# First layer's input projection from its second block on as three products of split operands, with both parts of the first norm counted together

## The reference, cut to what matters

```python
def rmsnorm(x, g, eps=NORM_EPS):
    xf = x.astype(jnp.float32)
    y = xf * lax.rsqrt(jnp.mean(xf * xf, axis=-1, keepdims=True) + eps)
    return (y * g).astype(x.dtype)

def even_mixer(hn, p, ctx, layer_idx):
    ...
    proj = hn @ p['w_in']                       # 1024 x (1536 + 352)
    qa, ka, va, q_down, ckv, kpe = jnp.split(
        proj, [HA * 2 * DA, 2 * HA * 2 * DA, A_COLS, A_COLS + Q_LORA, A_COLS + Q_LORA + KV_LORA], axis=-1)
    ...
    qb = heads(rmsnorm(q_down, p['q_norm']) @ p['w_uq'], HB)
    ckv = rmsnorm(ckv, p['kv_norm'])
    ...

def trunk_layer(h, cond, p, mixer, ctx):
    sh1, sc1, g1, sh2, sc2, g2 = jnp.split(jax.nn.silu(cond) @ p['ada_w'] + p['ada_b'], 6, axis=-1)
    hn = rmsnorm(h, p['norm1']) * (1.0 + sc1) + sh1
    m, ctx_out = mixer(hn, p['mix'], ctx)
    ...
```

## Time and profile before

| | |
|---|---|
| Time before, median of 3 runs | 2240.46 us (2232.99 to 2259.75) |
| Profiled execution, its own time | 2247.07 us |
| Its span in the trace | 2245.3 us |
| PE busy | 2114.6 us, 94% of the span |
| DVE busy | 1097.4 us, 49% |
| ACT busy | 659.0 us, 29% |
| DMA queue of weight loads, share of 16 engines | 20.6% |

### The profile page before, as it was taken

The page is one execution under the profiler, slowest core; times in us unless marked ns, Lnnn a source line. Parts: engine busy times, 40 slices in busy tenths (PEclk is TensorE's granted clock), DMA queues, the critical chain, the costliest instruction groups (busy, mean ns, idle before and its releaser), DMA issues.

```text
span 2245.3 us, 41199 instructions
## 1 busy us (share of the span) xinstructions
PE 2114.6 (94%) x18328; PEld 1776.9 (79%) x18328; DVE 1097.4 (49%) x2006; ACT 659.0 (29%) x1192; POOL 152.2 (7%) x145
## 2 busy tenths in 40 slices
PE   6998999999999999999998879999969999999998
PEld 3544444559999999999996468888945999999998
DVE  3004644426555554244544746777742655555423
ACT  2001433314333333132334423233111333333311
POOL 2000000000000000000002712222000000000000
PEclk8998999999999999999998869999979999999999
DMA  9021643712222211232120000000021222222222
GB/s 325 26 75 57 216 151 113 262 38 76 76 76 76 76 52 53 78 94 76 57 66 7 20 2 3 3 4 3 4 80 38 75 71 74 76 73 59 54 78 73
DMA packets 141505, 163.72 MB, mean 73 GB/s; under 512 B 2368, under 2 KB 106864, under 8 KB 141328
## 3 DMA queue, kind: packets, MB, share of 16 engines
q1 hardware_dynamic: 137872, 148.81, 20.6%
q0 software_dynamic: 3456, 12.28, 1.6%
HBM read 157.32 MB, written 3.75 MB: 72 GB/s over the span
## 4 chain that ended last, share of the span: by engine, by line
PE 87%; DVE 8%; DMA 2%; ACT 1%; issue 1%; POOL 0%; ACTq 0%; SPq 0%; DVEq 0%; POOLq 0%
PE ps L218 82%; DMA ring<-in_ada_w 1%; PE ps L1619 1%; PE ps L1034 1%; DVE work L2160 1%; DMA ring<-in_ffn_up 1%; PE ps L314 1%; DVE work L463 1%; DVE x_lo_r L469 0%; DVE work L2205 0%; PE ps L329 0%; PE ps L1937 0%; PE ps L1919 0%; PE ps L427 0%; DVE work L2196 0%
## 5 line engine op out<-in xcount | busy, mean ns | idle before, releaser
L218 PE MATMUL ps<-x_hi_r,w_lo 128*128 128x320 f32 (+2 forms) x2112 | 497.2, 311 | 4.5 <-ACTq L202 3.5
L218 PE MATMUL ps<-work 64*64 64x64 f32 (+6 forms) x4942 | 388.0, 272 | 31.0 <-ACT work L2080 9.1
L218 PE MATMUL ps<-x_lo_r,w_hi 128*128 128x320 f32 (+2 forms) x1664 | 394.1, 311 | 8.2 <-DVE g_lo L737 8.2
L218 PE MATMUL ps<-x_hi_r,w_hi 128*128 128x320 f32 (+2 forms) x1664 | 393.5, 310 | 0.7 <-issue 0.7
L218 PEld LDWEIGHTS ps<-work 64*64 64x64 f32 (+4 forms) x4942 | 249.4, 150 | 158.7 <-issue 101.0
L218 PEld LDWEIGHTS ps<-x_hi_r,w_lo 128*128 128x128 f32 x2112 | 357.4, 188 | 6.4 <-ACTq L202 3.7
L218 PEld LDWEIGHTS ps<-x_lo_r,w_hi 128*128 128x128 f32 x1664 | 283.2, 189 | 8.8 <-DVE g_lo L737 8.8
L218 PEld LDWEIGHTS ps<-x_hi_r,w_hi 128*128 128x128 f32 x1664 | 281.7, 188 | 1.2 <-issue 1.1
L568 DVE SCALAR_TENSOR_TENSOR work<-ps,par,work 128x511 f32<-128x511 f32 (+1 forms) x188 | 103.4, 550 | 272.3 <-ACT work L702 264.6
L615 DVE TENSOR_TENSOR w_lo<-ring,w_hi 128x1024 fp32r<-128x1024 f32 (+1 forms) x152 | 158.4, 1078 | 98.5 <-ACT w_hi L604 98.5
L702 ACT ACTIVATE work<-ps,par 128x640 f32<-128x640 f32 x88 | 77.8, 884 | 400.8 <-PE ps L218 400.8
(11 more groups left out here) (332 smaller groups left out, 2355.0 us busy)
## 6 DMA issues: line engine op xcount, KB each, us to landing
ring<-in_ada_w SPq DMA_DIRECT2D x24, 2048.0 KB, 8.1
ring<-in_ffn_up SPq DMA_DIRECT2D x44, 1024.0 KB, 7.2
ring<-in_ffn_down SPq DMA_DIRECT2D x16, 1408.0 KB, 7.0
ring<-in_l_w_in SPq DMA_DIRECT2D x11, 1024.0 KB, 5.2
ring<-in_l_w_out SPq DMA_DIRECT2D x4, 2048.0 KB, 9.1
ring<-in_l_w_in SPq DMA_DIRECT2D x3, 2048.0 KB, 7.9
h<-in_xT POOLq DMA_DIRECT2D x1, 2560.0 KB, 14.8
out_yT<-work POOLq DMA_DIRECT2D x2, 768.0 KB, 4.2
```

The source lines that it names most:

```text
L218: return pe.matmul(out, lhsT, rhs, start=first, stop=last)
```

## The change

Block 0 stays as it is. Blocks 1, 2 and 3 are made of three fp32r products each. For that, ACT copies the eight tiles of `hn` to `x_hi` right behind the norm, and DVE, once block 0 is done, subtracts to `x_lo` in place over `hn`; each of the three weight blocks is rounded by ACT in four pieces (`m0_w_hi`) and subtracted by DVE in four (`m0_w_lo`), at places written out in `mix0_act` and `mix0_dve`. The hi weights lie in three areas of `work` that the attention uses later. Since `merged` now holds `x_hi`, the latent `ckv` is copied straight to its place in `ckv_b` in two pieces, normed there in two pieces, and the two copies at the end of `mix0_dve` go. The two parts of the first norm (latent and context tokens) now count one semaphore (`hn_ready`) together, and the counts that later parts wait for are moved by the eight tiles and twelve pieces that this stage adds.

```diff
-                act.activation(hn(t, 0, NL), hn(t, 0, NL), ACT.Identity, bias=shift(t, 0)).then_inc(sg("hn_half"), 1)
+                act.activation(hn(t, 0, NL), hn(t, 0, NL), ACT.Identity, bias=shift(t, 0)).then_inc(sg("hn_ready"), 1)
                 act.activation(hn(t, NL, NT), hn(t, NL, NT), ACT.Identity, bias=shift(t, 1)).then_inc(sg("hn_ready"), 1)
...
+        def m0_w_hi(act, j, part):
+            i, w = m0_block[j], m0_w(j) // 4
+            if part == 0:
+                act.wait_ge(full[i % RING], 16 * parts_before[i % RING][i + 1])
+                if j >= 2:
+                    act.wait_ge(*released[m0_block[j - 2]])
+                if j == 3:
+                    act.wait_ge(*released[m0_block[1]])
+            at = SLOT * (i % RING) + w * part
+            act.activation(m0_hi[j][:, w * part:w * part + w], ring[:, at:at + w], ACT.Copy).then_inc(sg("in_hi"), 1)
+
+        def m0_w_lo(dve, j, part):
+            w = m0_w(j) // 4
+            dve.wait_ge(sg("in_hi"), 4 * (j - 1) + part + 1)
+            at = SLOT * (m0_block[j] % RING) + w * part
+            dve.tensor_tensor(wl_b[:, at:at + w], ring[:, at:at + w], m0_hi[j][:, w * part:w * part + w].bitcast(F32),
+                              ALU.subtract).then_inc(sg("in_lo"), 1)
...
+            for j, cuts in ((1, [(P * m, P * m + P) for m in range(4)]), (2, ((0, 128), (128, 192), (192, 320), (256, 352)))):
+                next_block(pe)
+                pe.wait_ge(sg("in_lo"), 4 * j)
+                wh, wl = m0_k3(m0_hi[j][:, :]), m0_k3(m0_lo(j))
+                for c0, c1 in cuts:
+                    pe.wait_ge(sg("m0_copied"), n - 2)
+                    x_ready = (lambda k: pe.wait_ge(sg("x_lo"), k + 1)) if n == 4 else None
+                    project_split(pe, n % 3, lambda k: wh[:, k, c0:c1], lambda k: wl[:, k, c0:c1], xh, xl, KT, x_ready, c1 - c0)\
                         .then_inc(sg("m0_prod"), 1)
                     n += 1
                 released.append((sg("m0_prod"), n))
...
             for tt in range(5):
                 pe.wait_ge(sg("m0_copied"), n - 2)
                 for k in range(KT):
-                    ins = mm(pe, bank(2 * (n % 3)), hn(k, P * tt, P * tt + P), w[:, k, :], k == 0, k == KT - 1)
+                    for x, w in ((xh, wh), (xl, wh), (xh, wl)):
+                        ins = mm(pe, bank(2 * (n % 3)), x(k, P * tt, P * tt + P), w[:, k, :], k == 0 and x is xh and w is wh,
+                                 k == KT - 1 and w is wl)
...
         def mix0_act(act):
             n = 0
+            for t in range(KT):
+                act.wait_ge(sg("hn_ready"), 2 * t + 2)
+                act.activation(xh(t), hn(t), ACT.Copy).then_inc(sg("x_hi"), 1)
             for m in range(8):
...
+                if m in (0, 1, 4, 5):
+                    for part in range(2 * (m % 2), 2 * (m % 2) + 2):
+                        m0_w_hi(act, 1 + m // 4, part)
...
+                if i in (0, 1):
+                    for part in range(2 * i, 2 * i + 2):
+                        m0_w_hi(act, 3, part)
...
         def mix0_dve(dve, ch):
+            for part in range(4):
+                m0_w_lo(dve, 1, part)
+            dve.wait_ge(sg("m0_prod"), 4)
+            for t in range(KT):
+                dve.wait_ge(sg("x_hi"), t + 1)
+                dve.tensor_tensor(xl(t), hn(t), xh(t).bitcast(F32), ALU.subtract).then_inc(sg("x_lo"), 1)
+            for j in (2, 3):
+                for part in range(4):
+                    m0_w_lo(dve, j, part)
             for m in range(9):
...
-            ch(dve.tensor_copy(ckv_b[:, 0:NL], merged(0, 0, NL)))
-            ch(dve.tensor_copy(ckv_b[:, KP0:NK], merged(0, NL, NT)))
```

77 lines of the change are left out of this document (46 added, 31 removed).

## The result

The changed kernel took 2232.62 us (median of 20 runs, 2217.77 to 2258.65). The kernel before, in 20 runs beside it, took 2251.36 (2232.99 to 2259.75). The ratio is 0.9933, with an interval of 0.9915 to 0.9952: 15.1 us less of 2251.36, between 10.8 and 19.1. That is no change by the bound of 2%, and a small gain by the interval. The forecast was 2221, so it was 11.6 us too low, and the range 2207 to 2236 holds the time. (Runs over 1.5% above the fastest of their kernel, the longest of these 20 among them, are left out of every ratio and of the table of all timed runs.)

What follows compares the result with a forecast made beforehand. PE's time for its columns was taken as the bound. Gains of 6.4, 6.7, 7.1 and 0.7 us, less 1.2, 0.1 and 0.2, gave 19.4 off 2240.46: 2221 us, range 2207 to 2236.

Steps and rivals of the forecast that it cites:

- What bounds the stage: Whole stage: bound by how long PE needs for its columns; 82% of the span is the matmul helper's line.
- column of blocks 1 and 2: Blocks 1 and 2: a split column takes 7.04 us instead of 8.65; gains 6.4 and 6.7 us.
- 512-wide fp32r matmul: Block 3: 0.227 us each, from the line through the measured widths 256, 320 and 384.
- value product: Block 3: 24 fp32r matmuls take 5.4 us instead of 6.87; five products gain 7.1 us.
- price of the seam: Between blocks 0 and 1: PE waits 1.2 us for the first tile of x_lo only.
- The supply: Split weights for blocks 1 to 3: ready before PE needs them, 13 us early for block 1, 9 to 10 later.
- Rival 4: Seams before blocks 2 and 3: split weights late by more than 9 us; 2225 to 2230 us, chance 3%.
- Rival 2: Block 3: a 512-wide fp32r matmul costs 0.43 us, like a fp32 record; 2245 us, chance 3%.
- Rival 1: Seam of blocks 0 and 1: PE idles 4.1 us and the clock falls to 0.50; 2225 us, chance 7%.
- The base: Whole kernel before: its median of 2240.46 us, from which 19.4 us are taken.
- So the gain should be handed on whole: Phases behind the stage: nothing tied to absolute time, so all 19.4 us reach the end.
- Rival 3: Later phases: shifted clock falls, eight times 1.5 us, leave 7 us of the gain; 2233 us, chance 8%.

Runs made afterwards that it cites:

- e4: Changed kernel, but PE waits for all eight tiles of x_lo before block 1; ratio 0.9978 to the kernel before, median 2243.84 us.
- e12: Kernel before, all products in fp32, with only ckv put straight in its place and its two end copies gone; ratio 1.0026, median 2256.24 us.
- e11: e5 with two needless DVE copies before lambda, 0.92 us together; ratio 0.9858 to the kernel before, median 2215.82 us.
- e5: Changed kernel with columns 1 to 3 of block 0 split too; ratio 0.9861 to the kernel before, median 2218.67 us.
- e10: Changed kernel with four needless DVE copies before lambda, so attention starts 1.84 us later; ratio 0.994 to the kernel before, median 2231.85 us.

## Why the prediction was right, and where it was wrong

**What bounds the stage, and the terms of its sum: right.** 19.4 us were forecast, 18.0 measured.

| term | forecast | measured |
|---|---|---|
| column of blocks 1 and 2 | 7.04 us | 7.04 |
| 512-wide fp32r matmul | 0.227 us | 0.227 to 0.23 |
| value product | 5.4 us | 5.47 |
| product with two rotations | 7.1 us | 7.21 (144.37 to 151.58) |
| price of the seam | 1.2 us | 1.24 (8.28 - 7.04) |
| attention's first matmul | 192.7 | 192.26, after a start 1.9 us earlier |

DVE's two copies of `ckv` are gone. The 1.4 us that are missing are in the main not in a term but in the clock. Block 0 took 0.4 us more (37.4 in place of 37.0). And the first value product after the small norms starts at half clock, so with its rotations it gained nothing: 170.72 to 180.29, 9.57 us, where the kernel before has 9.59:

```profile
188.31 2.88 PE L218 MATMUL ps<-work 128*128 128x512 f32 x4
191.03 7.03 PE L218 MATMUL ps<-ring,work 128*128 128x512 f32 x16
197.90 1.88 PE L218 MATMUL ps<-work 128*128 128x512 f32 x4
```

The sum had 1.4 for it; the seam and the end of the stage came out 0.4 better together. Its first three matmuls take from 173.36 to 175.42, 2.06 us, where behind an earlier rotation they take 1.10 (145.69 to 146.79); before, the low stretch ended at 190.3, ahead of that product (191.03). The extrapolation along the line through 256, 320 and 384 columns held.

**The supply: right.** The covers of 13 and 9 to 10 us were forecast and are 13 and 9.8. Rival 4 is out. **Rival 2** is out: 0.227 us and not 0.43. **Rival 1** is out for this seam, and `e4` shows that it would have come with an idle time of 6 us.

**The base: wrong, and most of the miss.** The step was to take the median of three runs, 2240.46, as the kernel's time, and to take 19.4 from it. Twenty runs gave 2251.36, and 63 later ones have a mean of 2248.4. That is 10.9 of the 11.6 us of the miss. The runs of before were known to reach from 2232.99 to 2259.75, and the profiled execution, with the trace on which every term stood, took 2247.07. The prediction widened the range for this, and the range held; the likeliest value could have been put between the two numbers. The ratio doesn't suffer from it.

**"So the gain should be handed on whole": wrong.** The argument was that nothing in the later phases is tied to absolute time. That holds for loads and waits, and the traces show no new wait. It doesn't hold for the clock. In three traces each, the attention took 235.8 to 237.9 us before and 244.5 to 246.9 after, with the same instructions. The three spans of the changed kernel are 10.9 us shorter than those of before in the mean: the stage gives 18.1, the attention takes 8.2, the rest gives 1.4 and the parts ahead of the stage take 0.4. In the timed runs the loss to the clock is smaller, about 4 us over the whole kernel (15.1 against the 19.1 at equal clock); the runs of before weren't all as short as its three traces. Rival 3 had this as a mechanism, at 8% and with eight falls of 1.5 us; the price (12 us) was too high against the 8 of the traces and the 4 of the timed runs, and it isn't many short falls but one low stretch of 27 us in one place. The estimate took its size from the 3 us of the earlier trace rows, and the low stretches of the attention before, 26 us in all, would have been the nearer row.

That the position of the clock's fall goes with the length of the attention is shown in seventeen traces, and most plainly by `e12` (0.9 and 0.4 us in the stage, an attention 3 to 13 us longer, no gain in time) and by `e11` (two copies before the attention, and the pattern of the kernel before is back). It isn't a rule by which one can place a stretch. `e5`, `e10` and `e12` each showed two patterns in two traces, and the forecasts of time that were built on it are not confirmed: that for `e10` (0.990) lies outside the measured interval, that for `e11` at its edge, and for `e12` the interval holds the rival's too. What sets, in one execution, where the first stretch starts, stays open. So does whether `e11` is faster than `e5`: 0.9858 against 0.9861, with intervals of some 0.004 to each side.

**The best version** here is `e5` with or without the two copies: 0.986, where the changed kernel has 0.9933. By its timed runs it is faster than both kernels, though by less than 2%. Its mean lies 12.6 us below the changed kernel's; 4.8 of that are the columns of block 0 that the change left in fp32, 1.5 less time at 0.50 in the stage, and most of the rest went with a higher mean clock (0.9605 against 0.9562), of which six runs don't say whether it stays.

## What to carry to other kernels

A product in fp32 that is bound by PE can be replaced by three in fp32r, and the gain can be worked out from rows of other widths to within a few tenths of a microsecond, if the first tile of the lo operand is all that PE waits for. What such a gain is worth at the end is only known to some 5 or 10 us of the clock's doing, so read the granted clock of the phases behind the change, with the count of matmuls beside it, before a gain that is missing or extra is put down to the change. And take the base of a forecast from more than three runs, or from a value between them and the profiled one, when they lie 27 us apart.
